# First block's attention: the bias added on VectorE inside the search for the maximum

## What is computed

```
logits = q @ k.T * d ** -0.5 + bias          # bias by distance (32 buckets)
logits = where(mask, logits, -1e30)
m = max(logits)                              # with the sink, where there is one
p = where(mask, exp(logits - m), 0)
out = (p / max(sum(p), 1e-30)) @ v
```

## Time and profile before

| | |
|---|---|
| median of 3 runs | 3310.24 us (3301.04 to 3315.97) |
| profiled execution | 3309.41 us, span 3307.6 us |
| PE busy | 3145.8 us, 95% of the span |
| PEld busy | 2559.3 us, 77% |
| DVE busy | 1950.1 us, 59% |
| ACT busy | 1320.3 us, 40% |
| mean granted clock of TensorE | 0.973 |

### The profile page before, as it was taken

How to read it: one execution, slowest core, us unless ns; L and a number is a source line. 1 busy time by engine, 2 the same in 40 slices (tenths; PEclk the granted TensorE clock), 3 DMA queues, 4 the chain that set the end, 5 groups by cost and what they waited for, 6 DMA issues and landing times.

```text
span 3307.6 us, 38824 instructions
## 1 busy us (share of the span) xinstructions
PE 3145.8 (95%) x14876; PEld 2559.3 (77%) x14876; DVE 1950.1 (59%) x2641; ACT 1320.3 (40%) x2024; POOL 235.1 (7%) x313
## 2 busy tenths in 40 slices
PE   8999999999999999999999999999993998989988
PEld 6887888888888888888878777777772887767666
DVE  5677555568768888798567333343443235455555
ACT  4443444443444443444542223333332224344553
POOL 1000000010011010101000000000002000110000
PEclk9999999999999999999999999999995999999999
DMA  8987855468767878897636423323423333564563
GB/s 237 339 268 255 276 154 174 137 204 267 265 213 260 271 239 268 217 310 252 203 103 216 136 77 103 103 82 120 137 89 147 108 100 96 181 206 141 188 241 134
DMA packets 318853, 621.51 MB, mean 188 GB/s; under 512 B 29436, under 2 KB 96377, under 8 KB 316749
## 3 DMA queue, kind: packets, MB, share of 16 engines
q1 hardware_dynamic: 296684, 544.74, 51.2%
q0 software_dynamic: 17584, 59.48, 5.1%
q10 hardware_dynamic: 4400, 14.81, 1.2%
HBM read 575.62 MB, written 49.61 MB: 189 GB/s over the span
## 4 chain that ended last, share of the span: by engine, by line
PE 86%; DVE 5%; DMA 3%; ACT 2%; issue 2%; POOL 1%; SPq 0%; ACTq 0%; POOLq 0%; DVEq 0%
PE acc L526 25%; PE acc L531 24%; PE acc L530 24%; PE acc L1230 4%; PE acc L1257 3%; PE acc L1245 2%; DMA raw<-in_w_in 2%; DVE w_lo L435 1%; PE acc L497 1%; PE acc L870 1%; PE acc L1234 1%; PE acc L1214 1%; ACT w_hi L429 1%; PE acc L558 0%; PE acc L777 0%
## 5 line engine op out<-in xcount | busy, mean ns | idle before, releaser
L526 PE MATMUL acc<-w_hi,a_hi 128*128 128x512 f32 (+4 forms) x3800 | 1514.2, 398 | 35.2 <-DVE w_lo L435 15.5
L531 PE MATMUL acc<-w_hi,a_lo 128*128 128x512 f32 (+4 forms) x3800 | 1477.7, 389 | 0.0
L530 PE MATMUL acc<-w_lo,a_hi 128*128 128x512 f32 (+4 forms) x3800 | 1476.9, 389 | 0.0
L435 DVE TENSOR_TENSOR w_lo<-raw,w_hi 128x1024 fp32r<-128x1024 f32 (+3 forms) x826 | 984.4, 1208 | 473.1 <-ACT w_hi L429 454.4
L429 ACT ACTIVATE w_hi<-raw 128x1024 fp32r<-128x1024 f32 (+3 forms) x826 | 855.4, 1046 | 853.2 <-PE acc L531 787.4
L526 PEld LDWEIGHTS acc<-w_hi,a_hi 128*128 128x128 f32 x3800 | 724.2, 191 | 186.2 <-DVE w_lo L435 28.1
L531 PEld LDWEIGHTS acc<-w_hi,a_lo 128*128 128x128 f32 x3800 | 723.0, 190 | 146.2
L530 PEld LDWEIGHTS acc<-w_lo,a_hi 128*128 128x128 f32 x3800 | 724.4, 191 | 131.7 <-issue 1.0
L1367 DVE TENSOR_REDUCE at_st<-acc 128x1 f32<-128x256 f32 (+3 forms) x208 | 101.2, 487 | 428.4 <-PE acc L1230 283.7
L1290 ACT ACTIVATE pb<-acc,at_st 128x256 f32<-128x256 f32 (+3 forms) x208 | 108.5, 522 | 377.1 <-DVE at_st L1367 353.7
L470 DVE SCALAR_TENSOR_TENSOR lanes_b<-raw,ct,lanes_b 128x1024 f32<-128x1024 f32 x150 | 190.3, 1310 | 0.7 <-DMA raw<-in_w_mod 0.7
(11 more groups left out here) (375 smaller groups left out, 1856.7 us busy)
## 6 DMA issues: line engine op xcount, KB each, us to landing
raw<-in_w_mod SPq DMA_DIRECT2D x192, 512.0 KB, 5.0
raw<-in_w_mlp_in SPq DMA_DIRECT2D x128, 512.0 KB, 4.2
raw<-in_w_mlp_out SPq DMA_DIRECT2D x128, 512.0 KB, 5.4
raw<-in_e_w_in SPq DMA_DIRECT2D x104, 512.0 KB, 5.2
raw<-in_w_in SPq DMA_DIRECT2D x96, 512.0 KB, 4.6
raw<-in_w_in SPq DMA_DIRECT2D x88, 472.0 KB, 6.0
raw<-in_w_o SPq DMA_DIRECT2D x64, 512.0 KB, 4.7
raw<-in_o_w_in SPq DMA_DIRECT2D x64, 512.0 KB, 4.5
```

The lines of the kernel that those rows point to most:

```text
L435: nc.vector.tensor_tensor(w_lo[:, n % SPLITS, 0:size], raw[:, r % RAWS, 0:size], w_hi[:, n % SPLITS, 0:size].bitcast(F32), ALU.subtract)\
L526: nc.tensor.matmul(o, s.lhs(0, kt, tt), wh, start=kt == 0, stop=False)
L530: nc.tensor.matmul(o, s.lhs(0, kt, tt), wl, start=False, stop=False)
L531: last = nc.tensor.matmul(o, s.lhs(1, kt, tt), wh, start=False, stop=end)
```

## The change

The units of the first block no longer have a `bias`, so PE issues no bias product for them and signals after the logits alone. They carry the same slice of the bias tiles as `mask`. Where a unit has a mask, DVE does one operation in place of the reduction: it adds the mask to the logits, multiplies by -1, writes the result back over the logits in PSUM, and gives the minimum of what it wrote, which is the negated maximum. ACT's exponential reads these negated logits with a scale of -1. Units of the second block stay as they were.

```diff
-    def __init__(self, q, k, v, keys, out, bias=None, sink=None, coeff=None, add=False, gate=None):
+    def __init__(self, q, k, v, keys, out, bias=None, sink=None, coeff=None, add=False, gate=None, mask=None):
+        self.mask = mask
...
                             nc.scalar.activation(self.pb[:, v % self.npb, 0:w.keys], acc[:, 4 + v % 2, 0:w.keys], ACT.Exp,
-                                                 bias=st[:, 0:1], accum_out=st[:, 1:2]).then_inc(p_done, 1)
+                                                 bias=st[:, 0:1], accum_out=st[:, 1:2],
+                                                 scale=1.0 if w.mask is None else -1.0).then_inc(p_done, 1)
...
-                            m = at_st[:, v % 8, 0:1]
-                            ins = nc.vector.tensor_reduce(m, acc[:, 4 + v % 2, 0:w.keys], AX.X, ALU.max, negate=True)
+                            m, s_ = at_st[:, v % 8, 0:1], acc[:, 4 + v % 2, 0:w.keys]
+                            if w.mask is not None:
+                                ins = nc.vector.tensor_tensor_reduce(s_, s_, w.mask, -1.0, -2 * NEG, ALU.add, ALU.min, m)
+                            else:
+                                ins = nc.vector.tensor_reduce(m, s_, AX.X, ALU.max, negate=True)
...
-                    bb = lambda m: (bias1[m][:, g, 256 - L:256], 0)
+                    bb = lambda m: bias1[m][:, g, 256 - L:256]
...
-                        Unit(qa, [ckT[:, 0:cl]], [cvt[0:cl, :]], cl, o(0), (cb, 0), None, gV[:, qt, g:g + 1]),
-                        Unit(qa, [k1T[0][:, 0:L]], vt(0), L, o(0), bb(0), None, gate(1), True),
-                        Unit(qa, [k1T[1][:, 0:L]], vt(1), L, o(0), bb(0), None, gate(2), True),
-                        Unit([q1T[1][:, qt, g, :]], [k1T[2][:, 0:L]], vt(2), L, o(1), bb(1), sink1[:, g:g + 1]),
-                        Unit([q1T[2][:, qt, g, :]], [k1T[3][:, 0:L]], vt(3), L, o(2), bb(2))]
+                        Unit(qa, [ckT[:, 0:cl]], [cvt[0:cl, :]], cl, o(0), coeff=gV[:, qt, g:g + 1], mask=cb),
+                        Unit(qa, [k1T[0][:, 0:L]], vt(0), L, o(0), coeff=gate(1), add=True, mask=bb(0)),
+                        Unit(qa, [k1T[1][:, 0:L]], vt(1), L, o(0), coeff=gate(2), add=True, mask=bb(0)),
+                        Unit([q1T[1][:, qt, g, :]], [k1T[2][:, 0:L]], vt(2), L, o(1), sink=sink1[:, g:g + 1], mask=bb(1)),
+                        Unit([q1T[2][:, qt, g, :]], [k1T[3][:, 0:L]], vt(3), L, o(2), mask=bb(2))]
```

## The result

The changed kernel takes 3285.46 us (median of 5 runs, 3283.64 to 3292.91); the kernel before, 3309.58 (5 runs, 3301.04 to 3315.97). The ratio is 0.9936, with a 95% interval of 0.9914 to 0.9957: 0.64% faster, by 0.4 to 0.9%. The forecast was 3288. The profiled execution took 3284.51 us.

The account below looks back on a forecast made before the run. PE was taken to bound the kernel: 24.3 us of bias products less 1.9 lost at group ends gives 22.4 off 3309.41, 3287.0, or 3287.8 against the median, stated as 3288; range 3277 to 3302.

Parts of the forecast that it names:

- What bounds the stage: In the first block's attention PE is busy for 303.8 of 310 us, so work taken off it counts nearly in full.
- 24.3 us of bias products: First block: 160 bias products leave PE, priced by distances between starts, 0.43 us for 256 columns and 0.22 for others.
- The extra of the new operation, 0.15: DVE's new operation costs 0.15 us per unit more than the reduction, bounds 0 to 0.25, 12 us over 80 units.
- 22.4: Net gain forecast for the first block in us: 24.3 of removed products less 1.9 lost at gate-group ends.
- The rule of two instructions: From the Trainium skill: a VectorE operation that also writes out its accumulator is two instructions, putting the extra near 0.25 us.
- my high end: Upper bound for the new DVE operation's extra: 0.06 plus 0.19 for a separate accumulator read, 0.25 us.
- 1.9 us lost at four gate-group ends: At four ends one bias product and the extra are lost: 0.43 + 0.15 at two, 0.22 + 0.15 at two.
- A: Rival, chance 0.19: TensorE's clock or other stages take some gain; at clock 0.97 the region loses 8.7 us, giving 3296.5.
- B: Rival, chance 0.12: a dear new operation makes the DVE and ACT chain bind each step; gain gone near 1.1 us extra.
- its own sum: Excess of missing product plus extra over 80 distances: 6 us at 0.5 extra, 19 at 1.0, 48 at 1.6.
- C: Rival, chance 0.07: no extra and no loss at group ends, 24.3 us gained, 3286; favourable clock 3278.
- The model of distances: In each first-block unit, only what exceeds the distance from copy end to PE's product delays PE; 72 of 80 stay covered.

Follow-up runs that it names:

- product_only: Kernel before with the first block's bias products removed, no mask and the plain reduction kept (computes something else): 3281.27 us, ratio 0.9935 to the kernel before.
- long_only: Kernel before with the change made only for the 32 units of 256 keys: 3296.35 us, ratio 0.9973 to the kernel before.
- op_only: Kernel before with bias products kept on PE and DVE doing the new operation with zeros as mask: 3306.62 us against 3304.34, ratio 1.0008.

## Why the prediction was right

**What bounds the stage.** Right: PE does. The removed products came off the region, and the stages behind took the earlier start up. The whole profiled execution is 3309.41 - 3284.51 = 24.9 us shorter, and the region alone 24.0; the 1.7 us by which it began earlier are not the change's.

**24.3 us of bias products.** Right, a little low. The four places apart, the steps shortened by 0.45 us on average for 256 keys (29 steps), 0.24 for 128 (30) and 0.23 for the shortest (16), against 0.43, 0.22 and 0.22. With the 1.7 us of the next points added back, the gross gain is 24.0 + 1.7 = 25.7 us, 1.4 more than the sum. The same excess shows in `product_only` and, for 256 keys, in `long_only`, so the new operation has no part in it. About 1.0 us of it lies not in the units but in the gate projections between them: the distances between starts from one gate matmul of the region to the next instruction of the queue (to a gate matmul or a logits product, 833 of them) add up to 199.6 us before and in `op_only`, 199.2 in `long_only`, and 198.6 after and in `product_only`. The sum in the prediction had no term for this; why they stand closer I did not find.

**The extra of the new operation, 0.15.** Inside its bounds (0 to 0.25), and mis-sized: 0.07 us at the exponential. Both errors of size have the same direction, 1.4 and about 0.3 us, and make up the 1.6 between 22.4 and 24.0. The rule of two instructions held, and the price I had tied to it didn't follow: the read takes 142 ns, but the operation in front of it is shorter than my high end had it, and DVE's next operation starts with the read (both at 449.22). `op_only` puts the whole cost at 0.2 us of region, `product_only` at 0.3.

**1.9 us lost at four gate-group ends.** Right in place and size. The four steps lost their bias product and 0.09 to 0.10 us more: 0.43 + 0.09 and 0.43 + 0.10 for 256 keys, 0.22 + 0.09 twice for 128, 1.67 us in all. `product_only` shows it without the new operation: the steps lose their product and do not shorten. The prediction put the waits right but expected nothing new late, and one is: the first product with values of each pair now waits for its copy (0.31 us at 449.25, 0.05 in the pairs with 128 keys), in front of the wait for the evacuation, which stays at 0.18. PE's waits are 1.4 us, not 2; its "0.6 or so" for the kernel before should read 1.0 by its own rows.

**Of the rivals.** A: the granted clock of the region is 1.00 in the kernel after too, and the stretch behind keeps 0.99; thinning out the fp32 products cost no clock, and in none of the twelve traces does a stretch at the lower level lie in the region. The mean over the execution is 0.973 in both. B: its price was off by far (0.07 in place of 1.1), but its mechanism is real. The prediction had the gain gone at an extra near 1.1 us and 19 us lost at 1.0. With two reductions more (0.92 for 256 keys, less for shorter units) 13.2 us were lost and 0.23% of gain stood; with four more, 42.0 us, and the kernel was slower by 0.64%. Held against its own sum, B's way of adding up was good: with two more the extra is 0.8 us on the mean and 24.3 - 10.8 = 13.5 us of the 24.3 are gone (its sum: 12), with four more 1.5 us and 24.3 + 18.0 = 42.3 (its sum: between 32 at 1.3 and 48 at 1.6). C: "everything counts in full" was nearer in size (24.0) than the forecast's 22.4, but for another reason than C gave: the losses at the group ends were there, and the gross gain was larger.

What stays open: why the gate matmuls stand closer, how the delays of a pair add up, and whether anything behind the second block takes up what is gained there. The model of distances was right to about 2 us in 20 for the change itself; for two reductions more it gave 7 us where 13.2 were lost.

## What to carry to other kernels

If one engine is full and another idles before the operation that follows, moving an addition into that operation pays by the distance between starts on the full engine, not by the listed durations. Then look for the few places where the distance from a producer's end to its user is near zero: a part of the gain is lost there, and they can be counted in the trace before anything is built. When the difference wanted is a few us in 3300, compare the length of the stage in the traces, which repeated within 0.1 us here (269.2 and 269.3; 267.8 three times) while the times of one kernel's runs spread over 6 to 19 us. And look behind a wait that grows: in the second block one grew by 0.5 us, the clock was low behind it, and the step lacked 2.0 us.

## What the runs showed of the hardware that was not expected

- An operation of VectorE that adds, scales, writes back to PSUM and reduces is hardly dearer than the plain reduction: 432 against 424 ns for 256 elements, 299 against 291 for 128, 700 against 692 for 512. Its read of the accumulator is listed with 142 ns and delays what depends on it by about 0.07 us.
- A longer wait of TensorE can come with a lower clock behind it, and then costs more than itself. In the second block it waits 2.48 us in place of 1.99, and its granted clock is then 0.51 for 3.4 us in place of 1.00; the step lacks 2.0 us of what the removed product should bring, or 2.1, in three traces of three.
- The time at the clock's lower level differs between executions of one kernel, with PE as full in both. Between the first block's attention and the second's, the two traces of the changed kernel have 51.2 and 37.5 us at the lower level, and take 1591.4 and 1584.1 us: 7 us of scatter, enough to hide a gain of 5 us.
